# Centred layer norms: a late mean taken out of three tiles by GpSimd, and each tile's remainder right behind its scale

## The reference, cut to what matters

```
for l in range(DEPTH):
    h = hybrid_mixer(x, ...)
    x = layer_norm(ALPHA * x + h, ln1_g[l], ln1_b[l])
    h = memory_cross_attention(x, mem, ...)
    x = layer_norm(ALPHA * x + h, ln2_g[l], ln2_b[l])
    h = conv_ffn(x, ...)
    x = layer_norm(ALPHA * x + h, ln3_g[l], ln3_b[l])
```

## Time and profile before

| | |
|---|---|
| runs (us) | 3705.66, 3709.35, 3712.00; median 3709.35 |
| profiled execution (us) | 3711.7, its span 3709.9 |
| mean granted TensorE clock | 0.976 of 2.4 GHz |
| busy: TensorE, VectorE, ScalarE, GpSimd | 95%, 44%, 27%, 56% |
| HBM | 92 GB/s over the span |

### The profile page before, as it was taken

One profiled execution on the slowest core, in us unless ns is written; L12 is line 12 of the kernel. 1 busy time (PEld: TensorE's weight loads), 2 busy tenths in 40 slices (PEclk: granted clock), 3 DMA queues, 4 the chain that ended last, 5 costly groups with the idle time before them and its releaser, 6 DMA issues.

```text
span 3709.9 us, 45174 instructions
## 1 busy us (share of the span) xinstructions
PE 3533.9 (95%) x17597; PEld 2768.1 (75%) x17597; DVE 1633.8 (44%) x2485; ACT 1018.8 (27%) x1967; POOL 2072.9 (56%) x2138
## 2 busy tenths in 40 slices
PE   8999998999999999999998999997999899989998
PEld 6777777888777777778886767775888677668886
DVE  3564436755436553476554444234322233233222
ACT  2344224212223341432112454333111133211111
POOL 5444574767554446557764554442666544447664
PEclk9999999999999999999998999998999999989999
DMA  4222233665221214246642222211333222123332
GB/s 139 63 63 63 85 90 95 193 186 161 84 74 56 68 43 118 70 128 185 184 134 70 64 70 63 77 56 53 107 97 91 85 74 57 57 64 91 97 91 74
DMA packets 578940, 345.22 MB, mean 93 GB/s; under 512 B 16047, under 2 KB 562216, under 8 KB 578728
## 3 DMA queue, kind: packets, MB, share of 16 engines
q1 hardware_dynamic: 577432, 340.17, 31.5%
q10 hardware_dynamic: 1296, 2.16, 0.2%
HBM read 340.14 MB, written 2.14 MB: 92 GB/s over the span
## 4 chain that ended last, share of the span: by engine, by line
PE 87%; DVE 7%; ACT 4%; issue 2%; DMA 1%; SPq 1%; POOL 0%; DVEq 0%; ACTq 0%
PE gemm L228 23%; PE gemm L231 23%; PE gemm L234 23%; PE scores L310 6%; PE outs L310 6%; PE scores L1557 1%; PE gemm L265 1%; PE gemm L266 1%; PE gemm L267 1%; DVE x_t L1204 0%; DVE tiles L1201 0%; DVE tiles L1650 0%; ACT tiles L670 0%; PE scores L2354 0%; DMA w_raw<-in_w_in 0%
## 5 line engine op out<-in xcount | busy, mean ns | idle before, releaser
L207 POOL CAST w_high<-w_raw 128x512 fp32r<-128x512 f32 (+1 forms) x1067 | 696.2, 652 | 1521.5 <-PE gemm L234 1163.9
L209 POOL TENSOR_TENSOR w_low<-w_raw,w_high 128x512 fp32r<-128x512 f32 (+1 forms) x1067 | 1388.7, 1302 | 85.4
L228 PE MATMUL gemm<-x_high,w_high 128*128 128x512 f32 x2584 | 716.5, 399 | 24.8 <-ACT tiles L1256 5.0
L231 PE MATMUL gemm<-x_low,w_high 128*128 128x512 f32 x2584 | 695.0, 391 | 0.0
L234 PE MATMUL gemm<-x_high,w_low 128*128 128x512 f32 x2584 | 693.3, 390 | 0.0
L228 PEld LDWEIGHTS gemm<-x_high,w_high 128*128 128x128 f32 x2584 | 475.2, 189 | 133.1 <-issue 21.2
L231 PEld LDWEIGHTS gemm<-x_low,w_high 128*128 128x128 f32 x2584 | 486.3, 188 | 104.9
L234 PEld LDWEIGHTS gemm<-x_high,w_low 128*128 128x128 f32 x2584 | 486.1, 188 | 103.3
L228 PE MATMUL gemm<-split_tiles,w_high 128*128 128x512 f32 (+1 forms) x1456 | 392.0, 390 | 9.6 <-DVE tiles L1647 2.6
L231 PE MATMUL gemm<-split_tiles,w_high 128*128 128x512 f32 (+1 forms) x1456 | 380.5, 382 | 0.0
L234 PE MATMUL gemm<-split_tiles,w_low 128*128 128x512 f32 (+1 forms) x1456 | 378.9, 381 | 0.0
(11 more groups left out here) (351 smaller groups left out, 3647.5 us busy)
## 6 DMA issues: line engine op xcount, KB each, us to landing
w_raw<-in_mlp_w SPq DMA_DIRECT2D x112, 512.0 KB, 4.0
w_raw<-in_mod_w SPq DMA_DIRECT2D x96, 512.0 KB, 3.8
w_raw<-in_w_in SPq DMA_DIRECT2D x88, 512.0 KB, 3.8
w_raw<-in_f_w_up SPq DMA_DIRECT2D x88, 512.0 KB, 5.0
w_raw<-in_e_w_in SPq DMA_DIRECT2D x48, 512.0 KB, 3.9
w_raw<-in_f_w_down SPq DMA_DIRECT2D x32, 512.0 KB, 4.1
w_raw<-in_o_w_in SPq DMA_DIRECT2D x30, 512.0 KB, 3.9
w_raw<-in_w_branch SPq DMA_DIRECT2D x48, 256.0 KB, 2.6
```

The source lines that it names most:

```text
L207: me.pool.tensor_copy(WH[:, h, 0:n], W32[:, s, c0:c0 + n]).then_inc(sem["w_rounded"], 1)
L209: me.pool.tensor_tensor(WL[:, h, 0:n], W32[:, s, c0:c0 + n], WH[:, h, 0:n].bitcast(F32), ALU.subtract).then_inc(sem["w_split"], 1)
L228: me.pe.matmul(o, WH[:, h, (k - k0) * cols:(k - k0 + 1) * cols], src(k)[0], start=begin and k == 0, stop=False)
L231: me.pe.matmul(o, WH[:, h, (k - k0) * cols:(k - k0 + 1) * cols], src(k)[1], start=False, stop=False)
```

## The change

In ln2 and ln3 (`following` given: the weights of the pair that comes next): the pair's weights are fetched and split by a function of its own, `prepare_pair`, called within the norm ahead of the loop over tiles; behind the spreading TensorE makes the late mean a second time, into bank 1 of `scores`; ScalarE copies it to tile 13 of `tiles`, ahead of the first rounding in its queue; GpSimd subtracts it in tiles 5, 6 and 7 of `x_t` (`LATE` = 5), while VectorE centres tiles 0 to 4 only, and its scales of the last three tiles wait for GpSimd. In all norms with remainders: remainder j stands right behind scale j (and the centring that goes with it) as long as tiles are still centred by VectorE in the loop, and one tile behind after that. For tiles 0 to 7 VectorE's order in the loop is, with s for a scale, c for a centring and l for a remainder:

```diff
+LATE = 5
...
+        def prepare_pair(me, weights, K):
+            raw = [fetch(me, w, K * P, P) for w in weights]
+            step = HWIDE // P
+            me.prepared = []
+            for k0 in range(0, K, step):
+                piece = []
+                for s, landed in raw:
+                    h, rounded, split, done = split_piece(me, s, landed, k0 * P, step * P)
+                    me.raw_free[s] = ("w_split", split)
+                    piece.append((h, split, done))
+                me.prepared.append(piece)
+
         def unit_pair(me, weights, K, src, ready):
-            raw = [fetch(me, w, K * P, P) for w in weights]
+            if me.prepared is None:
+                prepare_pair(me, weights, K)
+            pieces, me.prepared = me.prepared, None
...
             fills[2]()
+            if following is not None:
+                prepare_pair(me, following, KD)
+                again, copied = me.tick("pe_step"), me.tick("act_step")
+                if me.pe:
+                    mm(me, Q[:, 1, :], M["mean"], total).then_inc(sem["pe_step"], 1)
+                if me.act:
+                    me.act.wait_ge(sem["pe_step"], again)
+                    me.act.activation(T[:, 13, :], Q[:, 1, :], ACT.Copy).then_inc(sem["act_step"], 1)
+                moved = me.tick("pool_step", KD - LATE)
+                if me.pool:
+                    me.pool.wait_ge(sem["act_step"], copied)
+                    for j in range(LATE, KD):
+                        me.pool.tensor_tensor(X[:, j, :], X[:, j, :], T[:, 13, :],
+                                              ALU.subtract).then_inc(sem["pool_step"], 1)
             if me.dve:
                 me.dve.wait_ge(sem["pe_step"], spread)
             me.x_ready = []
-            scaled = {}
+            scaled, behind = {}, []
+
+            def low_part(j):
+                me.x_ready.append(me.tick("dve_step"))
+                if me.dve:
+                    me.dve.wait_ge(sem["act_step"], scaled["h", j])
+                    me.dve.scalar_tensor_tensor(XL[:, j, :], t[:, j, :], b[:, j:j + 1], XH[:, j, :].bitcast(F32),
+                                                ALU.add, ALU.subtract).then_inc(sem["dve_step"], 1)
+
             for j in range(KD + 1):
                 if j < KD:
                     scaled[j] = me.tick("dve_step")
                     if me.dve:
-                        me.dve.wait_ge(sem["dve_step"], centred[j])
+                        if following is not None and j >= LATE:
+                            me.dve.wait_ge(sem["pool_step"], moved - KD + 1 + j)
+                        else:
+                            me.dve.wait_ge(sem["dve_step"], centred[j])
...
-                    if j + AHEAD < KD:
+                    if j + AHEAD < (KD if following is None else LATE):
                         centre_tile(j + AHEAD)
...
-                if j > 0 and not hand_over:
-                    me.x_ready.append(me.tick("dve_step"))
-                    if me.dve:
-                        me.dve.wait_ge(sem["act_step"], scaled["h", j - 1])
-                        me.dve.scalar_tensor_tensor(XL[:, j - 1, :], t[:, j - 1, :], b[:, j - 1:j],
-                                                    XH[:, j - 1, :].bitcast(F32), ALU.add,
-                                                    ALU.subtract).then_inc(sem["dve_step"], 1)
+                if not hand_over:
+                    if j < KD:
+                        behind.append(j)
+                    while len(behind) > (0 if j + AHEAD < (KD if following is None else LATE) or j == KD else 1):
+                        low_part(behind.pop(0))
```

More of the change, by code:

```diff
@@ L167, in __init__ @@
                 self.x_ready, self.x_done = None, 0
-                self.early, self.late = [], None
+                self.early, self.prepared = [], None
                 self.sp, self.pool, self.act, self.dve, self.pe = (eng if kind == k else None for k in
@@ L249, in unit_pair @@
                         me.pe.wait_ge(sem[me.bank_freed[bank][0]], me.bank_freed[bank][1])
-            for k0 in range(0, K, step):
-                slots, made = [], []
-                for s, landed in raw:
-                    h, rounded, split, done = split_piece(me, s, landed, k0 * P, step * P)
-                    me.raw_free[s] = ("w_split", split)
-                    slots.append(h)
-                    made.append(done)
+            for k0, piece in zip(range(0, K, step), pieces):
+                made = [done for h, split, done in piece]
                 if me.pe:
-                    me.pe.wait_ge(sem["w_split"], split)
+                    me.pe.wait_ge(sem["w_split"], piece[1][1])
                     for k in range(k0, k0 + step):
@@ L262, in unit_pair @@
                         for bank in range(2):
-                            wh = WH[:, slots[bank], (k - k0) * P:(k - k0 + 1) * P]
-                            wl = WL[:, slots[bank], (k - k0) * P:(k - k0 + 1) * P]
+                            h = piece[bank][0]
+                            wh = WH[:, h, (k - k0) * P:(k - k0 + 1) * P]
+                            wl = WL[:, h, (k - k0) * P:(k - k0 + 1) * P]
                             me.pe.matmul(G[:, bank, :], wh, hi, start=k == 0, stop=False)
@@ L555, in up @@
                     if q == 0:
-                        first_two = unit_pair(me, [wcols(a["f_w_up"], l, 0, KD, half * D_FF) for half in range(2)], KD,
+                        first_two = unit_pair(me, up_pair(l), KD,
                                               xs, me.x_ready)
@@ L592, in conv_ffn @@
             down(12, 22, 1.0)
-            centred_norm(me, c["ln3_g"], c["ln3_b"], 6, (lambda: None, lambda: None, lambda: None), l == DEPTH - 1)
+            centred_norm(me, c["ln3_g"], c["ln3_b"], 6, (lambda: None, lambda: None, lambda: None),
+                         even_pair() if l == DEPTH - 1 else mixer_pair(l + 1), l == DEPTH - 1)
         def norm_square(j):
@@ L681, in square_part, with centred_norm @@
                     last.then_inc(sem["pe_step"], 1)
-        def centred_norm(me, g, b, first, fills, hand_over=False):
+        def centred_norm(me, g, b, first, fills, following=None, hand_over=False):
             t, s_ = T2, scale_rows[:]
@@ L1011, in cross @@
             square_sums(me, 0, 5)
-            centred_norm(me, c["ln2_g"], c["ln2_b"], 5, (lambda: None, lambda: None, lambda: None))
+            centred_norm(me, c["ln2_g"], c["ln2_b"], 5, (lambda: None, lambda: None, lambda: None), up_pair(l))
         Y = T[:, 8:16, :]
@@ L1161, in modulation, with even_pair, odd_pair, mlp_pair @@
             me.modulated = post
+        def even_pair():
+            return [a["e_w_in_2"][0][:, c0:c0 + P].rearrange("(k p) n -> p k n", p=P) for c0 in (D + 8 * P, D + 12 * P)]
+        def odd_pair():
+            return [a["o_w_in_2"][0][:, c0:c0 + P].rearrange("(k p) n -> p k n", p=P)
+                    for c0 in (3 * D + 4 * P, 3 * D + 5 * P)]
+        def mlp_pair(layer):
+            return [a["mlp_w1_2"][layer][:, q * P:(q + 1) * P].rearrange("(k p) n -> p k n", p=P) for q in range(2)]
+        def mixer_pair(l):
+            return [wcols(a["w_in"], l, 0, KD, n * P) for n in (16, 17)]
+        def up_pair(l):
+            return [wcols(a["f_w_up"], l, 0, KD, half * D_FF) for half in range(2)]
         def pre_norm(me, s_):
@@ L1231, in mixer @@
             nsink, rq = st[:, 48:56], st[:, 16:48].rearrange("p (b h) -> p b h", b=NB)
-            first_two = unit_pair(me, [zi(16), zi(17)], KD, xs, me.x_ready) if me.x_ready else None
+            first_two = unit_pair(me, mixer_pair(l), KD, xs, me.x_ready) if me.x_ready else None
             if l == 0:
@@ L1884, in up @@
                     if q == 0:
-                        second = w1[:, P:2 * P].rearrange("(k p) n -> p k n", p=P)
-                        first_two = unit_pair(me, [w, second], KD, xs, me.x_ready)
+                        first_two = unit_pair(me, mlp_pair(layer), KD, xs, me.x_ready)
                     done = first_two[q] if q < 2 else unit(me, w, KD, xs, q % 2)
@@ L2030, in even @@
                 me.act.wait_ge(sem["dve_step"], me.tables_made)
[L2031 removed]
+            first_two = unit_pair(me, even_pair(), KD, xs, me.x_ready)
             firsts = [conv_first(8 + 4 * i, first_two[i], i) for i in range(2)]
```

5 lines of the change are left out of this document (2 added, 3 removed).

## The result

The changed kernel takes 3715.90 us (median of 11 runs, 3709.46 to 3721.34), the one before 3706.72 in 11 runs beside it (3703.65 to 3712.0). That is **9.2 us or 0.25% slower**: ratio 1.0027, 95% interval 1.0019 to 1.0035, which is 7.0 to 13.0 us. The profiled execution of the changed kernel took 3715.92 for a span of 3714.1, at a mean granted clock of 0.976, the same as before.

A forecast was written before the change was run, and what follows sets the result against it. The prediction took TensorE, busy for 95% of the span, to bound the kernel. Its terms, 6.6+0.7+0.8+1.3+0.3 = +9.7 us, on the median of 3709.35 gave 3719.05, forecast as 3719.0, range 3710 to 3726.

The forecast's parts named there:

- (1): ln1, both layers: the new order leaves the wait unused and remainders wait for roundings and splits; +3.3 us each.
- The loss without any hold: ln1: later end of the pair from the new order alone, with no collision with GpSimd; +1.9 us.
- the term of the splits' holds: ln1: GpSimd's splits of the next weights hold remainders 4, 5 and 6 by 0.4+0.4+0.6 us, all on the path.
- (2): ln2 twice, ln3 of layer 0: mean and copy delay the first rounding, 617.33 to 617.45 in ln2; 0.7 us in ln3.
- the forecast case: ln3 of layer 0: slow spreading, second mean ending near 1009.3, first rounding 0.7 us late.
- (3): ln2, ln3 of layer 0: GpSimd's subtractions hold remainders; ln2 +0.7 and +0.8 us, ln3 +1.3 us.
- the splits hold 5 to 7, the last coming at 632.0: ln2 of layer 0: GpSimd's weight splits delay remainders 5 to 7, the last coming at 632.0; part of +0.7 us.
- (4): ln3 of layer 1, without remainders: the copy delays ScalarE's first pass; +0.3 us, bounds 0 and 0.6.
- (5): Splitting the pair's weights earlier in the program text changes no queue; cost 0.
- (A): Rival, chance 0.27: collisions are cheap or miss each other; +2.7 us, 3712.
- (B): Rival, chance 0.15: the clock falls in ln1's new gaps; +3.4 to +6.8 us on top, 3722 to 3726.
- (C): Rival, chance 0.08: not slower, the second mean keeps TensorE at 2.4 GHz up to the pair; -5.2 us, 3704.

The follow-up runs named there:

- e1: Changed kernel with VectorE's old order in ln1 alone; 3707.13 us against 3705.07 for the kernel before, ratio 1.0006.
- e9: Changed kernel, but in ln1 GpSimd splits no next weights before the last remainder; one run of 3720.72 us against 3706.98 for the kernel before.
- e8: Changed kernel with scale 1 and centring 4 put back into ln1's wait; one run of 3710.80 us against 3706.08 for the kernel before.
- e4: Changed kernel without GpSimd's three subtractions, second mean and copy kept; 3708.38 us against 3705.07 for the kernel before, ratio 1.0008.
- e7: Changed kernel with nine GpSimd fills in place of its three subtractions; one run of 3706.45 us against 3706.08 for the kernel before.
- e5: Changed kernel with ln1's old order, no second mean, first mean copied early, GpSimd subtracting in two tiles; 3707.76 us against 3706.08 for the kernel before.
- e6: As e5, but GpSimd subtracts in three tiles; 3701.26 us against 3706.08 for the kernel before, ratio 0.9992.
- e3: Changed kernel with VectorE's old order in every norm, second mean, copy and subtractions kept; 3710.14 us against 3705.07 for the kernel before, ratio 1.0011.
- e2: Changed kernel with the new order everywhere but no second mean, copy or GpSimd subtractions; 3717.17 us against 3705.07 for the kernel before, ratio 1.0032.
- e10: As e6, but with VectorE's old order in all norms; 3708.97 us against 3706.98 for the kernel before, ratio 1.0002.

## Why the prediction was right, and where its terms were off

The forecast difference was +9.7 and the measured one +9.2 [7.0, 13.0]; the mechanism, a new order that leaves ln1's wait unused and holds that eat GpSimd's relief, is what the runs show. That the sum fits so closely is in part luck: the stretches of ln2 of layer 0 and ln3 of layer 1 missed by -1.2 and +1.4, which cancel. By its own steps:

**(1) ln1, +3.3 each: measured +2.75 and +2.76.** This carries 5.5 of the 8.65 us of stretches, and e1, with ln1's order alone undone, gives 7 of 9.2 back. The steps came out closely: 2.19 a tile was forecast and 2.20 measured, with the rounding 0.78 behind the scale and the same start of TensorE. Two terms were off and in part cancel. The loss without any hold was put at 1.9 and is 2.28 (e9). Too large was the term of the splits' holds, 0.4+0.4+0.6 with its knock-on. Remainder 4 was held 0.11 (0.86 long), and the last two took 1.83 together, about 0.4 over two free ones; e9, without any of these holds, is 0.47 shorter. I had placed the splits to a tenth from the trace of before, and they met the remainders elsewhere. Of the 2.75, then, 1.26 is the work that no longer fills the wait, as worked out in the forecast, about 1.1 is the wait of remainders 1 to 4 for their roundings (2.20 a tile, where scale, centring and remainder take 1.93), and 0.47 is holds; e8 gave back only 0.5, as most of the refilled 1.26 went into another wait and another hold.

**(2) Second mean and copy: right for ln2, a matter of the execution for ln3.** The copy takes 0.60, with 0.49 to the rounding, which comes 0.96 behind the scale; 0.90 was forecast and 0.78 was before. In ln3 of layer 0 it was to be 0.7 late because of a slow mean. In the profiled execution it was not: the first remainder came 1.70 behind scale 0, as in ln2. So the +1.54 beside the forecast +1.3 is luck: the start was 0.3 sooner than before, and some 12 of the pair's matmuls came 0.43 apart, before 6. e4 shows the forecast case (1.91 for the mean, the first remainder 1.25 later), e1 and e9 a case between (2.10 and 2.13), and the forecast had taken the clock of before for granted.

**(3) Holds by GpSimd's subtractions: shown, with one sum wrong.** TensorE was to start 0.2 sooner and did by 0.3. Remainders 0 and 1 were held 0.50 and 0.73. With the holds taken away (e4, e7) ln2 is 1.2 shorter, against 1.2 and 1.4 between the forecast with and without holds. But ln2 of layer 0 came out at -0.50 instead of +0.7. The term that was mis-sized is again the holds. Tile 0 was consumed as forecast, at 0.43 a matmul. But remainder 1 let TensorE go on at 626.31, 5.94 behind scale 0, where the forecast has 6.45, and "the splits hold 5 to 7, the last coming at 632.0", 15.45 behind scale 0, failed: the last remainder starts 13.68 behind it, held up by only 0.38 (remainder 6 is 1.13 long). So the pair's end was not set by the last tile, as forecast, but by TensorE's own pace, and that depends on the granted clock: 14 matmuls at 0.50 before, 7 after. Four executions of this same code (after, e1, e8, e9), with the last remainder at 13.52 to 13.69, gave 16.48, 16.44, 16.44 and 17.95; the forecast's 17.7 lies among them, but for another reason. ln2 of layer 1 (+0.40 against +0.8) and ln3 of layer 0 lie in a like spread (16.45 to 17.59, 16.83 to 17.81). That the place of the low-clock stretch makes this spread is read from the counts of matmuls 0.43 apart beside it (ln3 of layer 0: about 12 in the execution of 17.58, 4 in that of 16.83); no run moved it on purpose.

A size that the forecast nearly had: it took the 0.55 by which the addition of the earlier trace rows ends behind GpSimd, but then let a held remainder only start when the subtraction ends. In the traces a held remainder ends 0.55 behind the subtraction that holds it: at 626.26 behind 625.71 in ln2 above, and likewise in e5 (627.49 behind 626.94), e6 (617.53 behind 616.98), e3 (620.67 behind 620.12) and e8 (538.99 behind 538.44). Each such hold is thus 0.2 shorter than forecast.

**(4) ln3 of layer 1, +0.3: measured +1.70, a miss.** ScalarE's first pass came 0.89 later behind scale 0, outside the bounds of 0 and 0.6, because the spreading and the second mean ran slowly in this execution, which the forecast had reckoned with in ln3 of layer 0 only; 0.8 more came from the pair's matmuls. This term too varies by execution: with the same code in this norm e1, e3, e8 and e9 gave +1.71, +1.25, -0.04 and +1.33, the first pass coming 0.17 (e8) to 0.89 (e1) later. And with neither second mean nor copy in this place e2, e5, e6 and e10 started the pair as before (18.07 to 18.10 behind scale 0) and still took 0.35 to 0.98 more, so the kernel before had a short stretch here, and part of the +1.70 is that.

**(5) Earlier splits, 0: right.** GpSimd's subtractions start 6.23 after its last work, so it waits for the copy and not for the pair's weights.

**The rivals.** (A) Cheap collisions, +2.7: refuted by the two stretched remainders in ln2, and its 1.9 for ln1 without collisions by e9's 2.28. (B) A clock that falls in ln1's new gaps: refuted. Behind the first matmuls of the pair, which ran at the lower level before as well, the clock stayed at 1.00 through the gaps of 0.49 and 0.74 in layer 0:

```profile
545.00:556.50 11.50, 9.69 (x40) 6.71 (x39) 8.61 (x12) 7.06 (x11) 4.95 (x5) 1.00 0.04 11
```

In layer 1, and in e2, e4 and e7, which have the same ln1, between 1 and 8 of its matmuls came 0.43 apart, and its length stayed within 19.79 to 19.82: TensorE waits for tiles there whatever its clock. (C) A second mean that keeps the clock up: refuted in ln2 of layer 0, whose first seven matmuls ran at 0.50, and by the sign of the result.

**What stays open.** The stretches add up to +8.65, the medians to +9.2. Between the profiled executions the span differs by 4.2 only, since all that follows the last pair came out 5.7 shorter (1669.5 against 1675.2), with no edit there and the same 7644 matmuls. In the other timed kernels sum and difference of medians stand up to 3.1 apart, in both directions, so the sum of one execution stands for the median within some 3 us and not closer.

## What to carry to other kernels

Before an instruction is pulled ahead on an in-order engine, look for what the old order did in the waits: here a scale and a centring (1.26) filled a wait that the new order leaves empty, and each remainder then waited for its own rounding: with the holds 2.75 us twice, although no work was added in that norm. Moving work to a side engine costs least when it starts in a wait ahead of the critical stretch and ends before it: the same three subtractions cost 1.2 us a norm when they begin with the first rounding, and next to nothing when they begin 3 us earlier (e6). And relief and reordering are to be tried together as well as apart: the order alone (e2) and the relief alone (e3) were slower than before, early relief alone (e10) was no different from before, and early relief with the new order (e6) was the fastest kernel here.

## What the runs showed that was not expected

Taking one tile back from GpSimd (e5 against e6, two tiles instead of three) cost 2.4 us in each ln2, because two remainders came to start 0.02 and 0.03 behind a split's subtraction and were held about 1.1 each; 0.6 of VectorE's work moved the end by four times as much. A VectorE instruction that reads two SBUF tiles was never stretched by GpSimd's fills (0.75 beside 5.18 us of them), but by its subtractions to 0.93, 1.10, 1.23, 1.25, 1.48, 1.67 and 1.82. And an unchanged norm varies by up to 1.5 us between executions with its low-clock stretches: ln2 of layer 0 took 16.48 with seven matmuls at 0.50 and 16.44 in e8 with none 0.43 apart, where TensorE waited 1.23 and 0.54 for tiles instead of 0.43, so a few slow matmuls only fill such waits; with some 11 of them it took 17.95 in e9.
